# The MLP of a two-block layer kernel in seven block products instead of eight, with its activations and the residual kept in DRAM in between

## The reference, cut to what matters

```python
h = h + jnp.concatenate([attn_out, dn_out], axis=-1) @ w_o      # "wo"
m = rmsnorm(h, norm_mlp)
h = h + jnp.square(jax.nn.relu(m @ w_up)) @ w_down              # the MLP: 1024 -> 4096 -> 1024
gate = jax.nn.sigmoid(rmsnorm(h, norm_ple) @ w_ple_gate)        # "gate"
h = h + gate * (p @ w_ple_proj)                                 # "proj"
x = rmsnorm(h, norm_final)
```

## Time and profile before

| | |
|---|---|
| median of 3 runs | 2068.39 us (2067.29 to 2070.54) |
| the profiled execution, its span | 2079.0 us |
| PE busy | 2010.5 us (97%), 9957 matmuls |
| DVE busy | 976.0 us (47%) |
| ACT busy | 716.6 us (34%) |
| POOL busy | 370.9 us (18%) |
| DMA | 137.09 MB, 66 GB/s over the span |

### The profile page before, as it was taken

One profiled execution on the slowest core, in us unless ns is written; L12 is line 12 of the kernel. 1 busy time (PEld: TensorE's weight loads), 2 busy tenths in 40 slices (PEclk: granted clock), 3 DMA queues, 4 the chain that ended last, 5 costly groups with the idle time before them and its releaser, 6 DMA issues.

```text
span 2079.0 us, 24728 instructions
## 1 busy us (share of the span) xinstructions
PE 2010.5 (97%) x9957; PEld 1660.8 (80%) x9957; DVE 976.0 (47%) x1647; ACT 716.6 (34%) x1345; POOL 370.9 (18%) x437
## 2 busy tenths in 40 slices
PE   8989999989999999999999999999999999799999
PEld 7767788877778888888888888877988898567787
DVE  4556634455464333333333335445634447566641
ACT  5656212254343121211212114434121126455521
POOL 0042113740030000000000003354242216100100
PEclk9999999999999999999999999998999999899999
DMA  4143323211011111111111112111311132511123
GB/s 148 41 119 114 109 82 97 89 52 41 22 50 44 50 51 51 51 41 51 51 51 50 41 51 61 40 53 52 122 31 31 42 122 94 154 31 31 41 82 102
DMA packets 194122, 137.09 MB, mean 66 GB/s; under 512 B 34952, under 2 KB 180616, under 8 KB 193496
## 3 DMA queue, kind: packets, MB, share of 16 engines
q1 hardware_dynamic: 194008, 135.51, 21.8%
HBM read 108.17 MB, written 27.31 MB: 65 GB/s over the span
## 4 chain that ended last, share of the span: by engine, by line
PE 86%; DVE 6%; ACT 3%; POOL 3%; DMA 1%; issue 1%; SPq 0%; DVEq 0%; POOLq 0%
PE ps L338 22%; PE ps L339 22%; PE ps L340 22%; PE ps L351 4%; PE ps L2824 3%; PE ps L581 2%; PE ps L1297 1%; PE ps L2725 1%; PE ps L2813 1%; PE ps L2814 1%; PE ps L2815 1%; DVE gtmp L775 1%; PE ps L1281 1%; PE ps L2554 1%; DVE xl L1583 1%
## 5 line engine op out<-in xcount | busy, mean ns | idle before, releaser
L338 PE MATMUL ps<-xh,whi 128*128 128x512 f32 (+2 forms) x1728 | 689.3, 399 | 4.7 <-DVE xl L1583 3.2
L339 PE MATMUL ps<-xl,whi 128*128 128x512 f32 (+2 forms) x1728 | 667.5, 386 | 0.0
L340 PE MATMUL ps<-xh,wlo 128*128 128x512 f32 (+2 forms) x1728 | 666.3, 386 | 0.0
L338 PEld LDWEIGHTS ps<-xh,whi 128*128 128x128 f32 x1728 | 331.1, 192 | 69.8 <-issue 5.3
L340 PEld LDWEIGHTS ps<-xh,wlo 128*128 128x128 f32 x1728 | 330.2, 191 | 62.4
L339 PEld LDWEIGHTS ps<-xl,whi 128*128 128x128 f32 x1728 | 331.1, 192 | 57.8 <-issue 3.1
L317 ACT ACTIVATE whi<-wraw 128x1024 fp32r<-128x1024 f32 (+1 forms) x136 | 142.7, 1049 | 355.9 <-PE ps L340 340.9
L324 DVE TENSOR_TENSOR wlo<-wraw,whi 128x1024 fp32r<-128x1024 f32 (+1 forms) x136 | 181.0, 1331 | 97.0 <-ACT whi L317 96.8
L338 PE MATMUL ps<-ffh,whi 128*128 128x512 f32 x512 | 199.3, 389 | 0.0
L340 PE MATMUL ps<-ffh,wlo 128*128 128x512 f32 x512 | 199.2, 389 | 0.0
L339 PE MATMUL ps<-ffl,whi 128*128 128x512 f32 x512 | 199.2, 389 | 0.0
(11 more groups left out here) (441 smaller groups left out, 2528.7 us busy)
## 6 DMA issues: line engine op xcount, KB each, us to landing
wraw<-w_in SPq DMA_DIRECT2D x47, 512.0 KB, 3.9
wraw<-w_up SPq DMA_DIRECT2D x32, 512.0 KB, 4.0
wraw<-w_down SPq DMA_DIRECT2D x32, 512.0 KB, 3.4
xt<-x SPq DMA_DIRECT2D x8, 512.0 KB, 7.7
wraw<-w_o SPq DMA_DIRECT2D x8, 512.0 KB, 3.5
xr<-x SPq DMA_DIRECT2D x8, 512.0 KB, 3.7
wraw<-w_ple_gate SPq DMA_DIRECT2D x8, 512.0 KB, 4.2
h_d<-hT SPq DMA_DIRECT2D x8, 512.0 KB, 2.7
```

The source lines that it names most:

```text
L338: pe.matmul(out, h, xh[:, xk, c0:c1_], start=(n == 0), stop=False)
L339: pe.matmul(out, h, xl[:, xk, c0:c1_], start=False, stop=False)
L340: mm = pe.matmul(out, l, xh[:, xk, c0:c1_], start=False, stop=(n == nk - 1))
```

## The change

Both products of the MLP are cut into 2x2 blocks. Strassen's scheme forms sums of the blocks of either operand and needs seven block products where eight are needed otherwise; the order of the products is 1, 5, 2, 3, 7, 6, 4 (`ORDER`). The kernel computes them as follows.

* **Up.** 16 rounds q, each for 256 hidden features. A round has 7 products of 4 k x 3 = 12 matmuls, together 84 (16 rounds: 1344). POOL forms four weight sums of 128x512 and two output sums per round (`up_sum`, `up_pool`); ACT copies products 1, 5 and 7 out of PSUM; DVE makes the seven low parts and joins the outputs. The squared results go to DRAM (`ff_d`), four stores of 256 KB per round.
* **Down.** 4 groups g of 7 steps, each step with 4 tiles x 4 k x 3 = 48 matmuls (28 steps: 1344). A step's two operands, one quarter of `w_down` ("a") and one of `ff_d` ("b"), are 128x2048 and 1 MB each, loaded per step. DVE forms the sums a5, a7, a6 (`down_sum_dve`), POOL b5, b6, a3, b7, b4 (`down_sum_pool`), ACT the high parts (`down_high`) and DVE the low parts (`down_low`), all of 128x2048.
* **The residual** is saved to DRAM (`hm_d`) in the wo stage, its place is used for operands during up, and it is read back (8 x 512 KB) during the first steps of down.
* **The operands of up** (seven combinations of `hT`'s blocks) are made in the wo stage and right after it (`early_high`, `early_low`, `late_sum`, `late_low`).
* **Around it:** gate(0) takes its halves in the order 512, 0; the transposes of `p` move from the last down group to behind gate(0); `stats_pe` moves from behind gate(0) to the middle of gate(1); the first gate panel's load waits for the last group's product 5.

The diff, cut to its core:

```diff
@@ wo_act, wo_dve, wo_pool
+            if n % 2 == 1 and c0 == 0:
+                early_low(dve, w, n // 2)
+            if (n, c0) == (6, 512):
+                up_low(dve, w, 0, 1)
...
+    def late_low(dve, w, i):
...
+        dve.tensor_tensor(opL[i][:], opR[i][:], plain(opH[i]), ALU.subtract).then_inc(*dve_ml.up("x low", i))
...
+    def up_pe(pe, w, q):
+        for i in ORDER:
+            b = up_bank[i]
+            if i in FIRST:
+                out = take_bank(w, 4 * (q % 2) + b, (dve_ml, left[b]))
+            else:
+                out = bank[4 * (q % 2) + b]
+                w.wait_ge(*act_ml.at("s", q, {2: 1, 3: 5, 4: 7}[i]))
+            w.wait_ge(*dve_ml.at("w low", q, i))
...
+            if (q, i) == (0, 3):
                 stats_pe(pe, w, pe_ml, ("stats", "mlp"), accn, [pool_wo.end()], act_ml)
...
+    def up_dve(dve, w, q):
+        if q == 0:
+            up_low(dve, w, 0, 7)
+            late_low(dve, w, 6)
+            up_low(dve, w, 0, 6)
+            late_low(dve, w, 4)
+        up_low(dve, w, q + 1, 1)
+        if q == 0:
+            stats_dve(dve, w, act_ml, dve_ml, ("stats", "mlp"))
+            up_low(dve, w, 0, 4)
...
+    def down_first_sp(sp, w):
+        q = NP - 1
+        w.wait_ge(*pe_ml.at("up", q, 1))
+        down_load(sp, w, 0, "a", 1)
+        w.wait_ge(*pe_ml.at("up", q, 5))
+        down_load(sp, w, 0, "a", 5)
+        up_store(sp, w, q, 11)
+        w.wait_ge(*pe_ml.at("up", q, 2))
+        for i in (1, 7, 6):
+            down_load(sp, w, 0, "b", i)
+        w.wait_ge(*pe_ml.at("up", q, 3))
+        down_load(sp, w, 0, "b", 5)
+        for i in (7, 6):
+            down_load(sp, w, 0, "a", i)
...
+    def down_sp(sp, w):
+        for g in range(1, NG):
+            for i in ORDER:
+                w.wait_ge(*pe_ml.at("down", g - 1, i, 3))
+                for n in "ab":
+                    down_load(sp, w, g, n, i)
...
+    def down_low(dve, w, s, n):
...
+        if n == "a" and i == 5:
+            w.wait_ge(*dve_ml.at("d sum", g, 6))
+        if n == "a" and i == 6:
+            w.wait_ge(*pool_ml.at("d sum", g, "a", 3))
+        if n == "b" and i == 5:
+            w.wait_ge(*pool_ml.at("d sum", g, "b", 6))
+        if n == "b" and i == 6:
+            w.wait_ge(*pool_ml.at("d sum", g, "b", 4))
+        t = slot[n, i]
+        dve.tensor_tensor(t[:], slotR[n, i][:], plain(ring[n, s % 2]), ALU.subtract).then_inc(*dve_ml.up("d low", s, n))
...
+    def down_dve(dve, w):
+        for s, (g, i) in enumerate(down_steps):
+            last = s == NS - 1
+            down_read(dve, w, s - 1, 3)
+            if s == 0:
+                for k in (5, 7, 6):
+                    down_sum_dve(dve, w, 0, k)
...
+            down_low(dve, w, s + 1, "a")
+            down_read(dve, w, s, 0)
+            down_low(dve, w, s + 1, "b")
+            down_read(dve, w, s, 1)
+            if i == 6:
+                down_sum_dve(dve, w, g + 1, 5)
+            if i == 4:
+                for k in (7, 6):
+                    down_sum_dve(dve, w, g + 1, k)
+            down_read(dve, w, s, 2)
...
+    def down_pool(pool, w):
+        for g in range(NG):
+            for n, i in (("b", 5), ("b", 6), ("a", 3), ("b", 7), ("b", 4)):
+                down_sum_pool(pool, w, g, n, i)
...
     def mlp_pe(pe, w):
-        up_pe(pe, w, 0)
-        for g in range(NG - 1):
-            up_pe(pe, w, g + 1)
-            down_pe(pe, w, g)
-        down_pe(pe, w, NG - 1, lambda n: split_p_pe(pe, w, n // 2 - 1) if n in (3, 5) else None)
+        for q in range(NP):
+            up_pe(pe, w, q)
+        down_pe(pe, w)
...
     def ple_pe(pe, w):
         gate(0)
-        stats_pe(pe, w, pe_pl, ("stats", "ple"), acc1, [pool_pl.at("sum", 15)], act_pl)
+        for k in range(2):
+            split_p_pe(pe, w, k)
```

More of the change, by code:

```diff
@@ L1556, in sum_pool @@
             pool.tensor_tensor(acc, acc, sq[:], ALU.add).then_inc(*done.up("sum", i))
[L1560 to L1569, removed]
+    ORDER, FIRST = (1, 5, 2, 3, 7, 6, 4), (1, 5, 7, 6)
@@ new lines, in late_sum, with late_high @@
+    def late_sum(dve, w, i):
+        w.wait_ge(*pe_wo.end())
+        for j in range(4):
+            n = 2 * j if i == 7 else 2 * j + 1
+            w.wait_ge(*dve_ml.at("t2", j))
+            dve.scalar_tensor_tensor(opR[i][:, j], hT[:, n, 0:512], V("g_mlp")[:, n:n + 1], opR[6][:, j], ALU.mult, ALU.subtract
+                                     ).then_inc(*dve_ml.up("t late", i, j))
+    def late_high(act, w, i):
+        w.wait_ge(*dve_ml.at("t late", i, 3))
+        act.activation(opH[i][:], opR[i][:], ACT.Copy).then_inc(*act_ml.up("x high", i))
@@ L1595, in down_pe @@
[L1595 to L1636, removed]
-                dve.scalar_tensor_tensor(r[:], tile("up", g, f, c0), 0.0, RST[:, s], ALU.max, ALU.mult).then_inc(*dve_ml.up("ev", "up", g, f, c0))
-                w.wait_ge(*act_ml.at("ff high", g, f, c0))
-                dve.tensor_tensor(ffL[g % 2][:, f, s], r[:], ffH[g % 2][:, f, s].bitcast(F32), ALU.subtract).then_inc(*dve_ml.up("ff low", g, f, c0))
@@ new lines, in up_bank_of, with up_copy @@
+    def up_bank_of(q, i):
+        return bank[4 * (q % 2) + up_bank[i]]
+    def up_copy(act, w, q, i):
+        key = {1: "a", 5: "c", 7: 22}[i]
+        w.wait_ge(*pe_ml.at("up", q, i))
+        if q == 0 and i == 7:
+            w.wait_ge(*st_h.end())
+            w.wait_ge(*dve_ml.at("t late", 4, 3))
+        if q > 1:
+            if i == 1:
+                w.wait_ge(*dve_ml.at("t", q - 2, 21))
+                w.wait_ge(*pool_ml.at("c22", q - 2))
+            elif i == 5:
+                w.wait_ge(*pool_ml.at("s5 s7", q - 2))
+            else:
+                w.wait_ge(*st_ff[22][q % 2].at(q - 2))
+        act.activation(stage[key][q % 2][:], up_bank_of(q, i), ACT.Copy).then_inc(*act_ml.up("s", q, i))
@@ new lines, in up_relu @@
+    def up_relu(dve, w, q, c, src):
+        t = stage[c][q % 2][:]
+        if c in (12, 21):
+            w.wait_ge(*dve_ml.at("t", q, c))
+        elif c == 22:
+            w.wait_ge(*pool_ml.at("c22", q))
+        else:
+            w.wait_ge(*pe_ml.at("up", q, 2))
+            if q > 1:
+                w.wait_ge(*st_ff[11][q % 2].at(q - 2))
+        for c0 in (0, 512):
+            w.wait_ge(*dve_ml.at("rst", "stats", "mlp", c0))
+        dve.scalar_tensor_tensor(t, src, 0.0, RST[:, up_half[c]], ALU.max, ALU.mult).then_inc(*dve_ml.up("r", q, c))
@@ new lines, in down_high @@
+    def down_high(act, w, s, n):
+        if s >= NS:
+            return
+        g, i = down_steps[s]
+        if s > 1:
+            w.wait_ge(*pe_ml.at("down", *down_steps[s - 2], 3))
+        else:
+            w.wait_ge(*pe_ml.at("up", NP - 1, (5, 6)[s]))
+        if n == "a" and i in (5, 7, 6):
+            w.wait_ge(*dve_ml.at("d sum", g, i))
+        elif n == "a" and i == 3 or n == "b" and i in (5, 6, 7, 4):
+            w.wait_ge(*pool_ml.at("d sum", g, n, i))
+        else:
+            w.wait_ge(*(ld_a if n == "a" else ld_b)[i].at(g))
+        act.activation(ring[n, s % 2][:], slotR[n, i][:], ACT.Copy).then_inc(*act_ml.up("d high", s, n))
```

565 lines of the change are left out of this document (478 added, 87 removed).

## The result

The changed kernel takes 2086.15 us, the median of 10 runs, against 2072.45 for the kernel before (10 runs): ratio 1.006, 95% interval 1.0041 to 1.0078. It is slower by about 12 us (8.5 to 16 by the interval); 2078 had been forecast, or +9 to +10 on the kernel before. The stated range, 2018 to 2102, was wide enough to hold a gain as well, and slower had been given a chance of 0.48. Executions of one kernel spread over 13 us here, and much of that arises ahead of the MLP (the first wait of up came between 597 and 607 us in the traces), so I compare single traces inside one stretch only.

The account below looks back on a forecast made before the run. The prediction took the MLP to be bounded by matmuls alone. Its terms, -87.0 + 0 + 16 + 30 + 32 + 15 + 3 = +9, on 2068.4 gave 2077, plus 1 for small clock losses 2078 us; range 2018 to 2102.

Parts of the forecast that it names:

- Matmuls, -87.0: Up and down: 2688 matmuls instead of 3072, 384 fewer at 0.2267 us each, -87.0 us.
- the second rival: Rounds of up: late DMA or ACT's copy of product 1 leaves 1 us holes each round; 2100 us, chance 0.16.
- The turns of VectorE and GpSimd: Whole MLP: a VectorE instruction with both inputs in SBUF and a GpSimd instruction exclude each other; VectorE waits up to 4.3 us.
- The first rival: Up's entry through PLE: POOL's long sums don't hold DVE for their length; -44 us, 2024 us, chance 0.34.
- Boundaries, +32: Three down group boundaries: product 5 of the next group 9 us late plus 1.7 for the clock, three times, +32 us.
- Entry, +16: Start of up: product 4 of round 0 waits 15.6 us for DVE, plus 1.7 clock, less the old 0.95; +16 us.
- From up to down, +30: Start of down: step 0 is 4.2 us late, step 1 22, two falls of the clock 4; +30 us.
- Exit, +15: Down's end and gate(0): DVE and POOL need 44.5 us against PE's 21.8; two thirds of the missing 22.7 shows, +15.
- PLE, +3: PLE: reciprocals start later against gate(1)'s banks, so about one of 3.35 us shows; +3 us.
- The clock: Behind PE's waits: the granted clock falls to the lower level for some 3.3 us, costing 1.7 us.

Follow-up runs that it names:

- experiments 1 to 3: Changed kernel with GpSimd's five down sums per group moved to VectorE (ratio 0.9878), issued in four pieces (0.988), or computed on 16 columns (stretch 36.1 us shorter).
- experiment 6: Changed kernel with GpSimd's last four wo-stage sums of squares on 16 of 512 columns; one run, trace only: product 5's wait 3.1 us shorter.
- experiments 4 and 5: Changed kernel with VectorE's order at up's start altered (ratio 1.0085); the same plus product 5's low earlier and ScalarE's copies of products 1, 5, 7 ahead (1.0053).
- experiment 3: Changed kernel with GpSimd's five sums per down group computed on 16 of 2048 columns; one run, trace only: stretch 36.1 us shorter.
- Experiment 7: Changed kernel with the 16 sums of squares and 4 last additions at down's end moved from GpSimd to VectorE; ratio 1.0042 to the kernel before.
- experiment 10: Changed kernel with down and exit sums on VectorE, entry, loads and proj(0)'s split reordered, then three remaining waits mended; 2038.43 us, ratio 0.9813.

## Why the prediction was right

The mechanism is right: each of the losses is there, and where the working put it, save at the entry and in PLE. That the stretch came out at the very +9 of the sum is luck, since errors of 10 us either way cancel.

* **Matmuls, -87.0.** Right; the rounds of up have no hole, so the second rival is out.
* **The turns of VectorE and GpSimd.** Right, and the point on which it all rests. The rows showed them for instructions of 1.3 us, and by the Trainium skill ("SBUF — State Buffer", SBUF's two separate sides) the pair of ports is held for the whole instruction. The trace agrees at 4.6 us, and experiments 1 to 3 show it by three ways of taking it away. The first rival is out with them.
* **Boundaries, +32.** Three waits of 9 us were forecast, 9.2 were measured. With the clock they cost about 34, of which 6.8 is the clock (5.1 forecast).
* **Entry, +16.** 15.7 of waits, as worked out, but 10.7 of it at product 5 and only 3.3 at product 4, where I had put all. Product 5's weight low stands behind the early lows, each 1 us longer beside GpSimd (experiment 6); the working counted PE's demand for product 5 at 2.7 us and never held VectorE's list against it. At product 4 two lists wait for the same reciprocals, and I saw one: ScalarE's copy of product 7 was ready 1.7 us after the weight low (experiments 4 and 5).
* **From up to down, +30.** Step 0 waited 4.8 us (4.2 forecast), step 1 14.9 (22). The low part of b5, for which step 1 waits, was done 4 us sooner than worked out, because the working had one of GpSimd's turns too many: b7 came behind it and not ahead (the rows are in the last section). The other 3 us are no gain. Step 0 began 0.7 us later than forecast and, at the lower clock, took 2.5 longer, while VectorE's list went on; what the clock took there, the wait at step 1 did not. That the reread is hidden behind the late step 1 was right, and experiment 3 shows the price once it is not: 6.7.
* **Exit, +15.** 1.4 + 6.0 + 2.1 = 9.5 us. That two thirds of what the two engines lacked would show was a guess and too much. Experiment 7 gives exclusion some 4 of it; the other 5, left with GpSimd out of the exit, are VectorE's own list.
* **PLE, +3.** 3.9, but at proj(0)'s weights, whose low part stands behind the reciprocals, and not at a bank.
* **The clock.** Taken at 1.7 to 2 us a stall, from the one row of a wait of 2.3 us, behind six waits. There were nine of over 3 us, at 1.4 to 2.9 each: 20.7 in all (short waits included) against some 12 in the sum. The loss does not go by the wait's length: it was 2.0 behind the 14.9 us and 2.9 behind the second 9.2. The waits came out 10 us shorter than forecast (76.3 against about 87), the clock 9 us dearer. This is the cancellation. Only at step 0 of down are the two tied: what the clock cost there, step 1 had not to wait.

Open is what sets the clock's loss behind a wait: the 2.27 us before proj's weights, the same wait in both kernels, cost 1.6 us in the trace before and 0.1 in the one after. Nor was it tried whether an earlier landing of b1, from which VectorE's row starts, would shorten the 4.4 us of experiment 10. The 13 us by which executions of one kernel differ were not looked into.

## What to carry to other kernels

An engine's share of busy time says nothing of whom it locks out: work on the idle GpSimd can be dearer than the same work added to a busier VectorE, and where it must stay there, short instructions cost less than long ones. Count the operand sums and the operands' landing at the points where a new group starts, not per group. Before moving one wait, follow all in-order lists that stand behind the same event; with VectorE's and ScalarE's lists both behind one reciprocal, each mend only moved the hole to the next, and the gains of single experiments did not add.
